# Expert weights of a mixture-of-experts trunk: four buffers each, lower parts written over the loaded weights, 8 KB rows in place of 4 KB

## The chip, the cores and the metric

The kernel runs on one core of a Trainium2 chip. The metric is the time of one execution on the device in microseconds. Lower is better.

## The reference

One layer of a trunk over 512 positions of width 1024, all in float32. First a mixer (gated spatial mixing beside latent attention), then a mixture of experts. The change lies in the second part:

```python
def moe_ffn(h, w_router, router_bias, w_gate, w_up, w_down, ws_gate, ws_up, ws_down):
    ...                               # sigmoid scores, best 4 of 8 groups, then the best 8 of 64 experts per token
    combine = ...                     # (512, 64): weight of each expert for each token, zero where it isn't chosen
    routed = jnp.zeros_like(t)
    for e0 in range(0, N_EXPERTS, EXPERT_BLOCK):
        sl = slice(e0, e0 + EXPERT_BLOCK)
        hg = jnp.einsum('nd,edf->nef', t, w_gate[sl])
        hu = jnp.einsum('nd,edf->nef', t, w_up[sl])
        hw = jax.nn.silu(hg) * hu * combine[:, sl, None]
        routed = routed + jnp.einsum('nef,efd->nd', hw, w_down[sl])
    shared = (jax.nn.silu(t @ ws_gate) * (t @ ws_up)) @ ws_down
    return (routed + shared).reshape(B, S, D)
```

Each of the 64 experts has a gate and an up matrix of 1024 x 256 and a down matrix of 256 x 1024, 1 MB each, so 192 MB of weights are read once. With 8 experts for each of 512 tokens an expert has 64 tokens on average.

## The kernel before

The engines run programs of their own and meet at semaphores. The first part of the kernel (to about 300 us) is the mixer. Then comes the router on VectorE (DVE) with the shared expert between its steps, and then the expert loop, `every_expert`: four steps written out, a loop of 14 turns with four steps each, and four steps written out. A step handles expert E and prepares E+1 and E+2.

**Weights.** SyncE (SP) loads them, in the order of its program. For each expert there are six transfers of 512 KB: gate and up for the first four chunks of the contraction (half 0), gate and up for the other four (half 1), and two for down. Each fills 128 partitions with rows of 4096 bytes that are contiguous in memory. There are two buffers for each (`w_gu[half][i]`, `w_d[i]`). A load for E waits until VectorE has made the lower part of expert E-2, the last reader of the buffer (`gu_low_ok`, `d_low_ok`).

**Split operands.** A float32 product is made of three passes in a faster format. ScalarE (ACT) copies a weight to its high part (`gate_up_high`, `down_high`), VectorE subtracts it from the weight for the low part (`gate_up_low`, `down_low`, all through `lowered` at line 1503), and TensorE (PE) adds high x high, high x low and low x high (`three_passes`, lines 574 to 576). The high and the low parts have one buffer per half, and both engines wait for the matmuls that read it (`gu_mm0`, `gu_mm`, `d_mm`). Rows, hidden values and weights all go this way. Per expert VectorE makes six low parts of weights, two of rows (`xeT_low`) and one of hidden values (`hwT_low`), the gated product (line 1527) and two output pieces (`oute`, line 1539).

**Rows.** GpSimd (POOL) gathers an expert's token rows from memory by a list (line 524; `xe`, four buffers; up to 128 rows of 4352 bytes, the rest of the list out of bounds and skipped), and scatters the outputs with addition into the result (line 530; `oute`, two buffers; rows of 4096 bytes). Its program is: for each e, gather(e+3), wait for `oute_ok`, wait for `st_y` of all scatters before, scatter(e). As two experts may add to one row, a scatter begins only after the one before it has landed. Before the loop it also stores x, with the shared expert's output added, as the rows to add to (`st_x`).

**TensorE's step.** Transposes of the hidden values of E (line 827), `gate_up` for E+1, the transposes of the gathered rows for E+2 (`rows_T`, line 810), `down` for E.

Weights go through DMA queue q1 (SP's), gathers and scatters through q0 (POOL's), on the same 16 DMA engines.

Of the kernel before, what the change touches and what calls it, by code (L numbers as in the profile page):

```python
# [22 lines left out]
F32 = mybir.dt.float32  # L23
# [23 lines left out]
def trunk_kernel(nc, a, out):  # L47
# [31 lines left out]
    with ExitStack() as ctx:  # L79
# [106 lines left out]
        hwT_high = at("hwT_high", 183, [P, FC, P], F32R)  # L186
        hwT_low = at("hwT_low", 184, [P, FC, P], F32R)
# [14 lines left out]
        def small(name, shape, dt=F32):  # L202
# [63 lines left out]
        (consts, dve_step, pool_step, silu_c, rs_ok, col_ok, col_mm, ada_dve, acc_ok, ada_mm, mod_ok, g1_ok,  # L266
         g2_ok, ss_ok, std_ok, h_ok, hT_tr, hT_raw, hT_ok, wsT_tr, wsT_ok, proj_mm, proj_ok) = (sem(n) for n in (
            "consts", "dve_step", "pool_step", "silu_c", "rs_ok", "col_ok", "col_mm", "ada_dve", "acc_ok", "ada_mm",
            "mod_ok", "g1_ok", "g2_ok", "ss_ok", "std_ok", "h_ok", "hT_tr", "hT_raw", "hT_ok", "wsT_tr", "wsT_ok", "proj_mm", "proj_ok"))
        (stats_ok, vstats_ok, vstd_ok, lstd_ok, lrstd_ok, latn_ok, latT_tr, latT_ok, v_ok, gate_mm, gate_ok, kpe_ok, up_mm, up_ok, sq_ok,  # L270
         ssq_ok, qstd_ok, ang_ok, trig_ok, qk_ok, qkT_tr, qkT_ok) = (sem(n) for n in (
            "stats_ok", "vstats_ok", "vstd_ok", "lstd_ok", "lrstd_ok", "latn_ok", "latT_tr", "latT_ok", "v_ok", "gate_mm", "gate_ok", "kpe_ok",
            "up_mm", "up_ok", "sq_ok", "ssq_ok", "qstd_ok", "ang_ok", "trig_ok", "qk_ok", "qkT_tr", "qkT_ok"))
        (s_mm, nmax_ok, exp_ok, pT_tr, pT_ok, av_mm, o_ok, mix_v, oss_ok, ostd_ok, orstd_ok, mix_ok, mixT_tr, out_mm,
         x1_ok, ss2_ok, std2_ok, h2_ok, st_h2, h2T_tr, h2T_ok, rt_mm, sco_ok, selm_ok, pos_mm, lmat_ok, list_mm,
         list_ok) = (sem(n) for n in (
            "s_mm", "nmax_ok", "exp_ok", "pT_tr", "pT_ok", "av_mm", "o_ok", "mix_v", "oss_ok", "ostd_ok", "orstd_ok", "mix_ok",
            "mixT_tr", "out_mm", "x1_ok", "ss2_ok", "std2_ok", "h2_ok", "st_h2", "h2T_tr", "h2T_ok", "rt_mm",
# [5 lines left out]
        ld_gu = [[sem(f"ld_gu{half}_{i}") for i in range(2)] for half in range(2)]  # L284
        ld_d = [sem("ld_d0"), sem("ld_d1")]
# [10 lines left out]

        def num(E, d=0):
            m, r = E
            return r + d if m is None else m * 4 + (r + d)

        def pairs(E, d=0):

            m, r = E
            return r // 2 + 1 + d if m is None else m * 2 + (r // 2 + 1 + d)
# [12 lines left out]
        def first(E):  # L317

            return E[0] is None and E[1] == 0

# [54 lines left out]
        EXTRA0 = NE // 2  # L375
# [8 lines left out]
        def _(sp):  # L384
# [73 lines left out]
            def extra(i):  # L458
# [3 lines left out]
                load_gate_up(e, 0, 0)  # L462
                load_gate_up(e, 0, 1)
# [107 lines left out]
        def _(pe):  # L571
# [241 lines left out]
            def gate_up(i, n, before):  # L813
                pe.wait_ge(xe_low_ok, times(n, 2) + 2)
                wait(pe, hw_ok, before)
                for half in range(2):
                    pe.wait_ge(gu_low_ok[half], n + 1)
                    for c in range(HC):
                        last = three_passes(bank[2 + i][:], xeT_high[i][:, half * HC + c, :], xeT_low[i][:, half * HC + c, :],
                                            gu_high[half][:, :, c, :], gu_low[half][:, :, c, :], half == 0 and c == 0, half == 1 and c == HC - 1)  # L820
# [9 lines left out]
            def down(n):  # L830
# [3 lines left out]
                for m in range(2):  # L834
                    cols = slice(m * BANK, (m + 1) * BANK)
                    for j in range(FC):
                        last = three_passes(bank[4 + m][:], hwT_high[:, j, :], hwT_low[:, j, :], d_high[:, j, cols], d_low[:, j, cols], j == 0, j == FC - 1)
# [5 lines left out]
            def gate_up_of(E):  # L843
                gate_up(E[1] % 2, num(E), num(E, -1))
# [46 lines left out]
            def step(E):  # L891
# [6 lines left out]
                down(num(E))  # L898
# [3 lines left out]
            def extra(i):  # L902
# [4 lines left out]
                gate_up(0, n, n)  # L907
                hidden_T(0, n)
                down(n)
# [5 lines left out]
        def _(act):  # L915
# [20 lines left out]
            act.wait_ge(rs_ok, 1)  # L936
# [736 lines left out]
```

## Time and profile before

| | |
|---|---|
| median of 3 runs | 1065.07 us |
| lowest, highest | 1056.51, 1077.57 us |
| profiled execution, first to last instruction (span) | 1060.5 us |
| PE, DVE, ACT, POOL busy | 953.4, 880.5, 611.8, 273.5 us |
| moved by DMA | 286.27 MB, mean 270 GB/s |
| mean granted TensorE clock | 0.960 of full |

The profile is of one execution. Busy time is the time in which an engine works on an instruction. The chain of waits is followed back from the last instruction to what released it, step by step. "Idle before" is the engine's idle time just before an instruction, and the releaser is what ended it. The DMA share is the mean over the 16 DMA engines of the share of time in which they handle packets. It can be a little over 1, and a full one doesn't tell whether more bytes could move.

### The profile page before, as it was taken

The numbers are of one execution on the slowest core, as the hardware profiler recorded it, in microseconds if no ns is written. First come the engines' busy times: TensorE is split into PE (matmuls) and PEld (weight loads), VectorE is DVE, ScalarE is ACT, GpSimd is POOL, SyncE is SP. The second block draws the span as 40 slices with busy tenths as digits, with TensorE's granted clock in tenths as the row PEclk, the third lists the DMA queues.
The fourth block names the chain that finished last, engine by engine and source line by source line (L and its number), as shares of the span: only waits on it lengthen the run. The fifth ranks groups of instructions, "written<-read, shape, count | busy, mean of one in ns | idle before, by whom it ended". The sixth has DMA issues, their size and how long they took to land.

```text
span 1060.5 us, 14279 instructions
## 1 busy us (share of the span) xinstructions
PE 953.4 (90%) x4323; PEld 744.9 (70%) x4324; DVE 880.5 (83%) x1276; ACT 611.8 (58%) x961; POOL 273.5 (26%) x181
## 2 busy tenths in 40 slices
PE   1899999997999889999999999999998999899895
PEld 1654665876887568777778777787776777777773
DVE  4887775354548779999999999999998999999994
ACT  4215443554022157777777777776776777777672
POOL 1000205400000103242433423343333233333231
PEclk9899999588998999999999999999999999999998
DMA  9995222000044488999999999999999999999982
GB/s 351 396 381 206 80 79 109 1 1 1 40 178 184 132 308 286 368 368 340 342 357 344 370 352 342 361 349 359 322 345 353 314 345 365 360 359 352 358 290 48
DMA packets 93682, 286.27 MB, mean 270 GB/s; under 512 B 19497, under 2 KB 20009, under 8 KB 92753
## 3 DMA queue, kind: packets, MB, share of 16 engines
q1 hardware_dynamic: 71424, 248.04, 62.5%
q0 software_dynamic: 19056, 36.89, 13.9%
q10 hardware_dynamic: 3168, 0.94, 0.4%
q8 instruction: 16, 0.26, 0.1%
q14 instruction: 18, 0.14, 0.0%
HBM read 282.50 MB, written 37.88 MB: 302 GB/s over the span
## 4 chain that ended last, share of the span: by engine, by line
DMA 43%; PE 33%; DVE 11%; issue 8%; ACT 3%; POOL 1%; POOLq 0%; SPq 0%; DVEq 0%; ACTq 0%
DMA out<-oute,src_tab 31%; PE bank L613 9%; DMA xe<-h_rows,src_tab 6%; DMA w_gu<-in_w_exp_up 5%; PE bank L574 4%; PE bank L576 4%; PE bank L575 4%; DVE gu_low L1503 4%; PE bank L698 2%; PE bank L777 2%; PE bank L715 2%; DVE oute L1539 2%; POOL out L530 1%; DMA x_sb<-in_x 1%; PE bank L794 1%
## 5 line engine op out<-in xcount | busy, mean ns | idle before, releaser
L1503 DVE TENSOR_TENSOR gu_low<-w_gu,gu_high 128x1024 fp32r<-128x1024 f32 x256 | 301.6, 1221 | 9.7 <-ACT gu_high L1115 5.4
L1115 ACT CAST gu_high<-w_gu 128x1024 fp32r<-128x1024 f32 x256 | 256.7, 1055 | 76.4 <-PE bank L576 49.7
L530 POOL DMA_INDIRECT out<-oute,src_tab x64 | 133.2, 2081 | 426.7 <-DMA out<-oute,src_tab 291.1
L574 PE MATMUL bank<-gu_high,xeT_high 128*128 128x512 f32 x512 | 208.4, 407 | 4.5 <-DVE xeT_low L1503 4.2
L576 PE MATMUL bank<-gu_high,xeT_low 128*128 128x512 f32 x512 | 202.1, 395 | 0.0
L575 PE MATMUL bank<-gu_low,xeT_high 128*128 128x512 f32 x512 | 201.8, 394 | 0.0
L1503 DVE TENSOR_TENSOR d_low<-w_d,d_high 128x1024 fp32r<-128x1024 f32 x128 | 150.6, 1220 | 0.0
L1121 ACT CAST d_high<-w_d 128x1024 fp32r<-128x1024 f32 x128 | 128.3, 1056 | 12.9 <-PE bank L576 12.0
L574 PEld LDWEIGHTS bank<-gu_high,xeT_high 128*128 128x128 f32 x512 | 97.0, 189 | 26.3 <-issue 3.9
L574 PE MATMUL bank<-d_high,hwT_high 128*128 128x512 f32 x256 | 109.2, 427 | 6.7 <-DVE hwT_low L1503 6.5
L524 POOL DMA_INDIRECT xe<-h_rows,src_tab x64 | 100.6, 1571 | 53.2 <-DVE src_tab L1575 27.8
L576 PEld LDWEIGHTS bank<-gu_high,xeT_low 128*128 128x128 f32 x512 | 96.6, 189 | 22.4
L575 PEld LDWEIGHTS bank<-gu_low,xeT_high 128*128 128x128 f32 x512 | 96.9, 189 | 19.8 <-issue 0.2
L810 PE MATMUL bank<-ident,xe 128*128 128x128 f32 x512 | 70.8, 281 | 40.5 <-DMA xe<-h_rows,src_tab 38.4
L810 PEld LDWEIGHTS bank<-ident,xe 128*128 128x128 f32 x512 | 63.5, 192 | 58.7 <-issue 54.3
L576 PE MATMUL bank<-d_high,hwT_low 128*128 128x512 f32 x256 | 104.0, 406 | 0.0
L575 PE MATMUL bank<-d_low,hwT_high 128*128 128x512 f32 x256 | 102.9, 402 | 0.0
L1503 DVE TENSOR_TENSOR xeT_low<-bank,xeT_high 128x512 fp32r<-128x512 f32 x128 | 82.3, 685 | 21.4 <-ACT xeT_high L1131 20.2
L1131 ACT CAST xeT_high<-bank 128x512 fp32r<-128x512 f32 x128 | 68.8, 590 | 52.1 <-PE bank L810 50.0
L1539 DVE TENSOR_TENSOR oute<-bank,mod_rows 128x512 f32<-128x512 f32 x128 | 82.2, 685 | 8.6 <-PE bank L576 8.6
L574 PEld LDWEIGHTS bank<-d_high,hwT_high 128*128 128x128 f32 x256 | 50.3, 196 | 16.0 <-DVE d_low L1503 4.6
L576 PEld LDWEIGHTS bank<-d_high,hwT_low 128*128 128x128 f32 x256 | 49.7, 194 | 11.6
(283 smaller groups left out, 1277.1 us busy)
## 6 DMA issues: line engine op xcount, KB each, us to landing
w_gu<-in_w_exp_gate SPq DMA_DIRECT2D x128, 512.0 KB
w_gu<-in_w_exp_up SPq DMA_DIRECT2D x128, 512.0 KB
w_d<-in_w_exp_down SPq DMA_DIRECT2D x128, 512.0 KB
ada_w<-in_w_ada SPq DMA_DIRECT2D x8, 2048.0 KB
first_w<-in_w_ada SPq DMA_DIRECT2D x3, 2048.0 KB, 22.9
w_out_sb<-in_w_out SPq DMA_DIRECT2D x2, 2048.0 KB, 7.3
w_lat_sb<-in_w_in SPq DMA_DIRECT2D x1, 2688.0 KB, 23.2
x_sb<-in_x SPq DMA_DIRECT2D x1, 2048.0 KB, 13.7
```

The lines of the kernel that those rows point to most:

```text
L524: pool.indirect_dma_start(xe[i][:], None, h2_dram, bass.IndirectOffsetOnAxis(ap=rows, axis=0), bounds_check=last_row, oob_is_err=False).th ...
L530: pool.indirect_dma_start(out_rows, bass.IndirectOffsetOnAxis(ap=rows, axis=0), oute[i][:], None, bounds_check=last_row, oob_is_err=False, ...
L574: pe.matmul(dst, xh, wh, start=start, stop=False)
L575: pe.matmul(dst, xh, wl, start=False, stop=False)
L576: return pe.matmul(dst, xl, wh, start=False, stop=stop)
L613: last = pe.matmul(bank[2 + i % 4][:, 0:n1 - n0], hT[:, c, t * P:(t + 1) * P], w[:, c, n0:n1], start=(c == 0), stop=(c == C - 1))
L810: last = pe.transpose(bank[c // 4][:, c % 4 * P:(c % 4 + 1) * P], xe[b][:, c:D:C], ident[:])
L1115: act.copy(gu_high[half][:, m], w_gu[half][i][:, m]).then_inc(gu_high_ok[half], 1)
L1121: act.copy(d_high[:, m], w_d[i][:, m]).then_inc(d_high_ok, 1)
L1131: act.copy(xeT_high[i][:, m * HC:(m + 1) * HC, :], bank[m][:].rearrange("p (c n) -> p c n", c=HC)).then_inc(xe_high_ok, 1)
L1503: return dve.tensor_tensor(low, whole, high.bitcast(F32), ALU.subtract)
L1539: last = dve.tensor_tensor(oute[i][:, cols], bank[4 + m][:], mod[:, GATE2, cols], ALU.mult)
```

## The change

1. Each expert weight gets four buffers in place of two. One buffer `w_gu[i]` (16 KB per partition) holds gate and up whole; the four lie at 40, 56, 80 and 0 KB. The last is the place of x, so SyncE waits before the first load into it for the stores of x (`st_x`) and for the shared expert's last matmuls (`sd_mm`). `w_d[i]` lie at 72, 102, 120 and 175.5 KB. The one at 120 waits for `sgu_mm`, the one at 175.5 for `sd_mm`.
2. The low part is written over the loaded weight (`gu_low[i]` and `d_low[i]` have the addresses of `w_gu[i]` and `w_d[i]`), and the matmuls read it there. So a buffer is free only when the matmuls have read it: a load for E waits for `gu_mm` or `d_mm` of expert E-4.
3. Three transfers of 1 MB with rows of 8192 bytes per expert in place of six of 512 KB with rows of 4096 bytes.
4. VectorE no longer waits for `gu_mm0`, `gu_mm` and `d_mm` before a low part. The high parts keep one buffer per half and their waits.
5. To free semaphores, those of the square roots and reciprocals of the first part are merged into `std_ok` and `rstd_ok`, with the same order. TensorE's `gate_up` and `down` and the waits of ACT take the new buffer numbers (E % 4).

The core of the diff (left out: the merged semaphores, the numbers passed on, and the branch for more than 128 tokens in an expert):

```diff
         HC = C // 2
-        w_gu = [[at(f"w_gu{half}_{i}", 40 + 16 * half + 8 * i, [P, 2, HC, FF]) for i in range(2)] for half in range(2)]
-        w_d = [at(f"w_d{i}", 72 + 8 * i, [P, FC, D]) for i in range(2)]
-        gu_high = [at(f"gu_high{half}", kb, [P, 2, HC, FF], F32R) for half, kb in enumerate((16, 88))]
-        gu_low = [at(f"gu_low{half}", kb, [P, 2, HC, FF], F32R) for half, kb in enumerate((24, 102))]
+        D_AT = (72, 102, 120, 175.5)
+        GU_AT = (40, 56, 80, 0)
+        def gate_and_up(name, i, dt):
+            return at(f"{name}{i}", GU_AT[i], [P, 2, C, FF], dt)
+        w_gu = [gate_and_up("w_gu", i, F32) for i in range(4)]
+        gu_low = [gate_and_up("gu_low", i, F32R) for i in range(4)]
+        half_of = [slice(0, HC), slice(HC, C)]
+        w_d = [at(f"w_d{i}", kb, [P, FC, D]) for i, kb in enumerate(D_AT)]
+        d_low = [at(f"d_low{i}", kb, [P, FC, D], F32R) for i, kb in enumerate(D_AT)]
+        gu_high = [at(f"gu_high{half}", kb, [P, 2, HC, FF], F32R) for half, kb in enumerate((16, 24))]
         d_high = at("d_high", 112, [P, FC, D], F32R)
-        d_low = at("d_low", 120, [P, FC, D], F32R)
...
-            def load_gate_up(e, i, half):
+            def load_gate_up(e, i):
                 for m, w in enumerate(("w_exp_gate", "w_exp_up")):
-                    src = a[w][0, bass.ds(e, 1)].rearrange("o (p c) n -> p (o c) n", c=C)[:, half * HC:(half + 1) * HC, :]
-                    sp.dma_start(w_gu[half][i][:, m], src).then_inc(ld_gu[half][i], 16)
+                    src = a[w][0, bass.ds(e, 1)].rearrange("o (p c) n -> p (o c) n", c=C)
+                    sp.dma_start(w_gu[i][:, m], src).then_inc(ld_gu[i], 16)
             def load_down(e, i):
-                src = a["w_exp_down"][0, bass.ds(e, 1)].rearrange("o (p c) n -> p (o c) n", c=FC)
-                for j in range(FC):
-                    sp.dma_start(w_d[i][:, j], src[:, j]).then_inc(ld_d[i], 16)
+                sp.dma_start(w_d[i][:], a["w_exp_down"][0, bass.ds(e, 1)].rearrange("o (p c) n -> p (o c) n", c=FC)).then_inc(ld_d[i], 16)
             def down_step(E):
-                wait(sp, d_low_ok, num(E, -1))
+                wait(sp, d_mm, num(E, -3))
                 apart(sp, "sp")
-                load_down(num(E), E[1] % 2)
+                load_down(num(E), E[1] % 4)
             def step(E):
-                for half in range(2):
-                    wait(sp, gu_low_ok[half], num(E, -1))
-                    apart(sp, "sp")
-                    load_gate_up(num(E), E[1] % 2, half)
-                if not (E[0] is None and E[1] == 0):
+                if unrolled(E, 3):
+                    sp.wait_ge(sgu_mm, T)
+                    down_step((None, 2))
+                    sp.wait_ge(st_x, 16 * T)
+                    sp.wait_ge(sd_mm, T)
+                wait(sp, gu_mm, num(E, -3))
+                apart(sp, "sp")
+                load_gate_up(num(E), E[1] % 4)
+                if not (unrolled(E, 0) or unrolled(E, 3)):
                     down_step(after(E, -1))
...
             def gate_up_high(half, i, loads, n):
-                act.wait_ge(ld_gu[half][i], loads)
+                act.wait_ge(ld_gu[i], loads)
                 wait(act, (gu_mm0, gu_mm)[half], n)
                 for m in range(2):
-                    act.copy(gu_high[half][:, m], w_gu[half][i][:, m]).then_inc(gu_high_ok[half], 1)
+                    act.copy(gu_high[half][:, m], w_gu[i][:, m, half_of[half]]).then_inc(gu_high_ok[half], 1)
...
             def gate_up_low(half, i, n):
-                wait(dve, (gu_mm0, gu_mm)[half], n)
                 for m in range(2):
                     dve.wait_ge(gu_high_ok[half], times(n, 2) + (m + 1))
-                    last = lowered(gu_low[half][:, m], w_gu[half][i][:, m], gu_high[half][:, m])
+                    last = lowered(gu_low[i][:, m, half_of[half]], w_gu[i][:, m, half_of[half]], gu_high[half][:, m])
                 last.then_inc(gu_low_ok[half], 1)
             def down_low(i, n):
-                wait(dve, d_mm, n)
                 for m in range(2):
                     dve.wait_ge(d_high_ok, times(n, 2) + (m + 1))
-                    last = lowered(d_low[:, m], w_d[i][:, m], d_high[:, m])
+                    last = lowered(d_low[i][:, m], w_d[i][:, m], d_high[:, m])
                 last.then_inc(d_low_ok, 1)
```

## Rows read from the trace of the kernel before

**Rows 1.** Page, part 2: busy tenths of 40 equal slices.
```profile
DVE  4887775354548779999999999999998999999994
...
DMA  9995222000044488999999999999999999999982
```

**Rows 2.** Windows: busy us (instructions) of PE, PEld, DVE, ACT, POOL; PEclk, DMA share, GB/s.
```profile
500.00:620.00 120.00, 114.53 (x547) 93.41 (x547) 118.85 (x144) 90.46 (x131) 47.42 (x24) 1.00 1.00 354
...
740.00:860.00 120.00, 109.85 (x511) 89.39 (x509) 111.41 (x134) 84.82 (x123) 40.50 (x23) 0.97 0.99 335
860.00:980.00 120.00, 111.45 (x529) 91.20 (x529) 114.81 (x139) 86.95 (x128) 42.57 (x24) 0.99 1.02 358
```

**Rows 3.** Timeline of POOL: start us, us, instruction [idle before, releaser].
```profile
380.56 1.04 POOL L524 DMA_INDIRECT xe<-h_rows,src_tab  x1 [3.16 <-DMA out<-x_sb]
399.29 1.79 POOL L530 DMA_INDIRECT out<-oute,src_tab  x1 [17.68 <-DVE oute L1539]
...
604.92 2.87 POOL L530 DMA_INDIRECT out<-oute,src_tab  x1 [6.13 <-DVE oute L1539]
...
615.85 1.87 POOL L530 DMA_INDIRECT out<-oute,src_tab  x1 [6.00 <-DMA out<-oute,src_tab]
...
1028.94 1.84 POOL L530 DMA_INDIRECT out<-oute,src_tab  x1 [6.54 <-DMA out<-oute,src_tab]
...
1054.64 1.55 POOL L530 DMA_INDIRECT out<-oute,src_tab  x1 [6.87 <-DVE oute L1539]
```

**Rows 4.** Timeline of DVE: start us, us, instruction.
```profile
421.52 0.42 DVE L1503 TENSOR_TENSOR hwT_low<-bank,hwT_high 128x256 fp32r<-128x256 f32 x1
...
431.44 0.42 DVE L1503 TENSOR_TENSOR hwT_low<-bank,hwT_high 128x256 fp32r<-128x256 f32 x1
```

**Rows 5.** Waits, 400 to 1060 us: us in total, times, longest us.
```profile
POOL out L530 <- DMA out<-oute,src_tab: 291.1, 44, 8.4
POOL out L530 <- DVE oute L1539: 118.9, 18, 17.7
...
PE bank L810 <- DMA xe<-h_rows,src_tab: 38.4, 31, 3.2
...
ACT gu_high L1115 <- DMA w_gu<-in_w_exp_up: 20.3, 9, 3.1
```

**Rows 6.** Chain that ended last, in order of time: start us, us, what.
```profile
604.92 10.12 DMA out<-oute,src_tab
...
1011.32 18.25 DMA w_gu<-in_w_exp_up
```

**Rows 7.** Waits of SP's queue, 420 to 1060 us.
```profile
SPq L330 <- DVE gu_low L1503: 274.4, 114, 6.0
```

**Rows 8.** Windows of one us, at 309, 714, 715, 708 and 1058 us.
```profile
309.00:310.00 1.00, 1.00 (x11) 1.00 (x11) 0.96 (x2) 0.50 (x2) 0.00 (x0) 1.00 1.07 426
...
714.00:715.00 1.00, 1.00 (x6) 0.81 (x5) 1.00 (x2) 1.00 (x2) 0.00 (x0) 1.00 1.00 275
715.00:716.00 1.00, 1.00 (x6) 0.82 (x5) 1.00 (x2) 0.50 (x2) 0.00 (x0) 1.00 1.07 287
...
708.00:709.00 1.00, 1.00 (x6) 0.65 (x4) 1.00 (x2) 0.57 (x1) 1.00 (x1) 1.00 1.03 422
...
1058.00:1059.00 1.00, 0.00 (x0) 0.00 (x0) 0.00 (x0) 0.00 (x0) 0.00 (x0) 0.50 0.63 119
```

**Rows 9.** DMA view: packets of queue q0; issues of gathers and scatters.
```profile
q0 software_dynamic: 19056, 36.89, 13.9%
...
xe<-h_rows,src_tab POOLq DMA_INDIRECT x64
out<-oute,src_tab POOLq DMA_INDIRECT x64
```

**Rows 10.** Window from 332 to 358 us.
```profile
332.00:358.00 26.00, 23.10 (x85) 15.40 (x84) 19.63 (x56) 1.02 (x3) 1.27 (x2) 0.87 0.00 1
```

**Rows 11.** Timeline of SP's queue at the first load of expert 3.
```profile
380.48 0.33 SPq L435 DMA_DIRECT2D w_gu<-in_w_exp_gate  x1
```

More of the change, by code:

```diff
@@ L283, in trunk_kernel @@
             "sgu_mm", "ssilu_ok", "shw_ok", "shT_tr", "shT_ok", "sd_mm", "sh_ok"))
-        ld_gu = [[sem(f"ld_gu{half}_{i}") for i in range(2)] for half in range(2)]
-        ld_d = [sem("ld_d0"), sem("ld_d1")]
+        ld_gu = [sem(f"ld_gu{i}") for i in range(4)]
+        ld_d = [sem(f"ld_d{i}") for i in range(4)]
         ld_xe = [sem(f"ld_xe{i}") for i in range(4)]
@@ L319, in first, with unrolled @@
             return E[0] is None and E[1] == 0
+        def unrolled(E, r):
+            return E[0] is None and E[1] == r
         def wait(eng, s, value):
@@ L374, in trunk_kernel @@
         NI = T * H
-        EXTRA0 = NE // 2
+        EXTRA0 = NE // 4
         HW = HC // 2
@@ L828, in hidden_T, with down @@
                 last.then_inc(hwT_tr, 1)
-            def down(n):
+            def down(slot, n):
                 pe.wait_ge(d_low_ok, n + 1)
@@ L836, in down @@
                     for j in range(FC):
-                        last = three_passes(bank[4 + m][:], hwT_high[:, j, :], hwT_low[:, j, :], d_high[:, j, cols], d_low[:, j, cols], j == 0, j == FC - 1)
+                        last = three_passes(bank[4 + m][:], hwT_high[:, j, :], hwT_low[:, j, :], d_high[:, j, cols], d_low[slot][:, j, cols], j == 0, j == FC - 1)
                 last.then_inc(d_mm, 1)
@@ L897, in step @@
                     rows_T_of(after(E, 2))
-                down(num(E))
+                down(E[1] % 4, num(E))
             every_expert(pe, step)
@@ L985, in _ @@
             act.wait_ge(stats_ok, 1)
-            act.activation(latss[:, :, 0], latss[:, :, 0], ACT.Sqrt, bias=epsc[:], scale=1.0 / QL).then_inc(lstd_ok, 1)
-            act.activation(latss[:, :, 1], latss[:, :, 1], ACT.Sqrt, bias=epsc[:], scale=1.0 / KL).then_inc(lstd_ok, 1)
-            act.wait_ge(lrstd_ok, 1)
+            act.activation(latss[:, :, 0], latss[:, :, 0], ACT.Sqrt, bias=epsc[:], scale=1.0 / QL).then_inc(std_ok, 1)
+            act.activation(latss[:, :, 1], latss[:, :, 1], ACT.Sqrt, bias=epsc[:], scale=1.0 / KL).then_inc(std_ok, 1)
+            act.wait_ge(rstd_ok, RSTD_LAT)
             for t in range(T):
@@ L1015, in _ @@
             act.wait_ge(vstats_ok, 1)
-            act.activation(lnmv[:, :, 1], lnmv[:, :, 1], ACT.Sqrt, bias=epsc[:]).then_inc(vstd_ok, 1)
+            act.activation(lnmv[:, :, 1], lnmv[:, :, 1], ACT.Sqrt, bias=epsc[:]).then_inc(std_ok, 1)
             act.wait_ge(kpe_ok, T)
@@ L1035, in _ @@
             act.wait_ge(ssq_ok, 2 * T)
-            act.activation(qkss[:], qkss[:], ACT.Sqrt, bias=epsc[:], scale=1.0 / QD).then_inc(qstd_ok, 1)
+            act.activation(qkss[:], qkss[:], ACT.Sqrt, bias=epsc[:], scale=1.0 / QD).then_inc(std_ok, 1)
             act.wait_ge(g1_ok, 1)
@@ L1070, in _ @@
             act.wait_ge(oss_ok, 1)
-            act.activation(oss[:], oss[:], ACT.Sqrt, bias=epsc[:], scale=1.0 / GW).then_inc(ostd_ok, 1)
-            act.wait_ge(orstd_ok, 1)
+            act.activation(oss[:], oss[:], ACT.Sqrt, bias=epsc[:], scale=1.0 / GW).then_inc(std_ok, 1)
+            act.wait_ge(rstd_ok, RSTD_OUT)
             for t in range(T):
@@ L1081, in std2 @@
                 act.wait_ge(ss2_ok, t + 1)
-                act.activation(ss[:, t:t + 1], ss[:, t:t + 1], ACT.Sqrt, bias=epsc[:], scale=1.0 / D).then_inc(std2_ok, 1)
+                act.activation(ss[:, t:t + 1], ss[:, t:t + 1], ACT.Sqrt, bias=epsc[:], scale=1.0 / D).then_inc(std_ok, 1)
             for t in range(T - 1):
@@ L1143, in gate_up_high_of @@
             def gate_up_high_of(half, E):
-                gate_up_high(half, E[1] % 2, times(pairs(E), 32), num(E))
+                gate_up_high(half, E[1] % 4, times(fours(E), 32), num(E))
             def down_high_of(E):
-                down_high(E[1] % 2, times(pairs(E), 16 * FC), num(E))
+                down_high(E[1] % 4, times(fours(E), 16), num(E))
             def rows_high_of(E):
@@ L1252, in _ @@
             dve.tensor_scalar(turns[:], turns[:], -1.0, float(np.pi / 2), ALU.mult, ALU.add).then_inc(ang_ok, 1)
-            dve.wait_ge(std_ok, 1)
-            dve.reciprocal(ss[:], ss[:]).then_inc(rs_ok, 1)
+            dve.wait_ge(std_ok, STD_X)
+            dve.reciprocal(ss[:], ss[:]).then_inc(rstd_ok, 1)
             for n in range(1, ADA_FIRST):
@@ L1301, in _ @@
                     dve.tensor_copy(ws_raw[:], bank[6][:].rearrange("p (g n) -> p g n", g=GG)).then_inc(wsT_ok, 1)
-            dve.wait_ge(lstd_ok, 2)
-            dve.reciprocal(latss[:], latss[:]).then_inc(lrstd_ok, 1)
+            dve.wait_ge(std_ok, STD_LAT)
+            dve.reciprocal(latss[:], latss[:]).then_inc(rstd_ok, 1)
             for j in range(ADA_FIRST + T + 1, ADA):
@@ L1323, in _ @@
             last.then_inc(vstats_ok, 1)
-            dve.wait_ge(vstd_ok, 1)
+            dve.wait_ge(std_ok, STD_V)
             link(dve.reciprocal(lnmv[:, :, 1], lnmv[:, :, 1]))
@@ L1397, in _ @@
             outputs(T - 1)
-            dve.wait_ge(ostd_ok, 1)
-            dve.reciprocal(oss[:], oss[:]).then_inc(orstd_ok, 1)
-            dve.wait_ge(orstd_ok, 1)
+            dve.wait_ge(std_ok, STD_OUT)
+            dve.reciprocal(oss[:], oss[:]).then_inc(rstd_ok, 1)
+            dve.wait_ge(rstd_ok, RSTD_OUT)
             for t in range(T):
@@ L1424, in norm2 @@
             def norm2(t):
-                dve.wait_ge(std2_ok, t + 1)
+                dve.wait_ge(std_ok, STD_X2 + t)
                 link(dve.reciprocal(ss[:, t:t + 1], ss[:, t:t + 1]))
@@ L1542, in gate_up_low_of @@
             def gate_up_low_of(half, E):
-                gate_up_low(half, E[1] % 2, num(E))
+                gate_up_low(half, E[1] % 4, num(E))
             def rows_low_of(E):
```

50 lines of the change are left out of this document (24 added, 26 removed).

## The prediction

> **What bounds the kernel now.** I read the page first, then windows of the expert loop, then the waits, then the order of time on GpSimd, on VectorE and on TensorE. The expert loop is the long stage: its 64 scatters begin at 399.29 us, and the last of them ends the program [rows 3]. On the page two resources look full there: DVE shows nines, and so does DMA [rows 1]. Windows of 120 us between 500 and 980 make that finer: VectorE is busy for 111 to 119 us of each, and the DMA share stands at 0.99 to 1.02 while 335 to 358 GB/s move [rows 2]. Busy shares alone don't tell which one decides, so I went to the distances between starts.
>
> The 61 scatter starts from 399.29 to 1028.94 us are 60 intervals [rows 3]: 629.65/60 = 10.49 us per expert. VectorE by itself could do better: in a stretch in which nothing stalls it, one hwT_low starts 9.92 us after the one before [rows 4]. So about 0.57 us of each interval is not VectorE's. The waits say whose it is. The scatter waits for the scatter before it 44 times (291.1 us), and only 18 times for VectorE's result. TensorE waits for gathered rows 31 times (38.4 us). The weights are late only 9 times, 20.3 us on ACT [rows 5].
>
> The order on GpSimd shows the mechanism. Scatters add into the same output rows, so each one waits until the one before has landed; those at 604.92 and 615.85 us are 10.93 us apart, and the second was waiting for the first. The gather that feeds an expert three places later stands behind the scatter in the same program, so when the scatter is late the gather is too [rows 3]. There the chain of waits spends 10.12 us from a scatter's issue to its landing [rows 6]. At the end of the kernel, where no weights flow, the last scatter starts at 1054.64 us and the span ends at 1060.5 us, 5.86 us later. So the same transfer costs 4.26 us more beside the weight loads. This chain, not VectorE, is what sets the loop in 44 of its steps.
>
> **The change, part by part.** *Six transfers to three, 4 KB rows to 8 KB rows.* The bytes are the same, 3 MB per expert. SyncE issues three instructions fewer per expert, worth nothing: it waits 274.4 us in the loop for VectorE to free gate and up buffers alone [rows 7]. What a row costs on a DMA engine: at full rate 4 KB rows moved at 422 GB/s, 26.4 GB/s per engine, so 0.155 us each; the shared expert's 8 KB rows moved at 426 GB/s, so 0.308 us each [rows 8]. Per expert that is 48 x 0.155 = 7.44 us against 24 x 0.308 = 7.39 us of each engine: a gain of 0.05 us, even if the loads were what is late. A half-size transfer is thus no handicap once others stand behind it.
>
> The other side of the larger rows is who stands behind them. Scatter and gather go through GpSimd's queue q0, weights through q1, on the same 16 engines. The DMA view counts 19056 packets on q0 for 64 gathers and 64 scatters [rows 9] and the five plain stores that GpSimd issues: 143.3 per transfer, 9 per engine. How the two queues share an engine shows in the scatter's dip. A scatter alone moves 119 GB/s at a DMA share of 0.63, so 189 GB/s while busy, and one of its 4 KB rows takes 0.347 us. If one weight packet went between two scatter packets, a pair of 8 KB would take 0.502 us and the rate would be 261 GB/s; with two weight packets per scatter packet it would be 299, and with scatters let past 189. In the dip at 714 to 716 us, 275 and 287 GB/s are measured at a share of 1.00 to 1.07 [rows 8]. One for one is nearest. Then every q0 packet waits for one weight packet, and doubling that packet adds 9 x 0.153 = 1.37 us to each scatter, and as much to a gather.
>
> The Trainium skill (DMA: Bandwidth & Descriptors, the section Queues, rings and completion order) says the same: a DMA engine goes round its queues packet by packet, whatever a packet holds. It speaks against this change. By that rule the added wait is the same 1.37 us; by a split in bytes it would be nothing.
>
> Bounds of that price: below, 0 (the engine shares by bytes, or the wait lies elsewhere). Above, the whole excess of a scatter beside the loads doubles, 4.26 us (everything the loads do to it grows with their packet). I take 1.37 because the dip fits it. A relief comes off: the DMA share is about 1.0 of 10.49 us [rows 2]; with nearly the same work in 11.7 us it is about 0.88, so 12% of the packets meet no weight packet. Of 2 x 1.37 us this is 0.33. Net 1.04 us.
>
> It counts where a scatter waits for a scatter: 44 x 1.04 = 46 us. The 18 steps that wait for VectorE hide it in their slack; without that cover they would add up to 19 us more.
>
> *Four buffers per weight, lower parts over the loaded weights.* A gate/up load of an expert is released by the matmuls of the expert four back instead of by VectorE's low part of the expert two back; the down load likewise. That is about one step earlier. It can only repair waits for weights: 20.3 us on ACT, and those overlap the gathers' lateness. With 44 scatter-bound steps the gain is from 0 to 20 us; I take 0, as these steps stay bound. At the start two more loads (gate and up of expert 2, down of expert 1; 3 MB) go out in the pause from 332 to 358 us, in which 1 GB/s moves [rows 10]. Nobody waits for them in the first experts, so 0; at most the 3.15 MB/354 GB/s = 9 us that they take off the DMA engines later. Against it, expert 3's load now waits for x to be stored (GpSimd passes the same wait at 380.56 us [rows 3]) and for the shared expert's end. In the kernel before its first half was issued at 380.48 us [rows 11], so the time is the same, and the cost 0. Behind that wait in SyncE's queue stand only loads of expert 3 and later.
>
> *Removed waits on VectorE.* Its low parts no longer wait for the matmuls (gu_mm0, gu_mm, d_mm). The high part, for which VectorE waits anyway, still waits for the same matmuls, so nothing moves; VectorE's operations keep their count and sizes. Writing the result over one operand has no row here: bounded by nothing and, upwards, by one per cent of 6 x 1.2 us, 0.07 us per expert; taken as 0. The matmuls read low parts with another stride: 0, since their columns are as many. The merged semaphores (std_ok, rstd_ok) keep the same waits: 0.
>
> **The sum.** 1060.5 + 46 = 1106.5 us on the profiled execution's span. That span lies 4.6 us below the median of the runs, 1065.1 us. So 1111 us.
>
> **The rivals.**
> *Faster: DMA work, not latency, is the bound, and lead and larger rows buy it.* For: a DMA share near 1.0 in every window, 18.25 us from issue to landing for a load near the end [rows 6]. Against: the saving in engine time is 0.05 us per expert, and what is late in the middle is the gather. If it were so, VectorE's 9.92 us would be the floor: 60 x 0.57 = 34 us less, 1031 us. It decides only if q0's packets aren't delayed by more than 0.6 us per scatter. 15%.
> The Trainium skill (the same page, the section Bandwidth) advises transfers of 1 MiB and more for 75% of the peak; by that rule the new loads would be the better ones, and this rival would gain. The trace disagrees for queued loads: half-megabyte ones moved 422 GB/s.
> *No change: the engines share by bytes.* Then scatter and gather see the same wait, and the lead saves from 0 to 17 us: 1048 to 1068 us. For: the rates of the dip lie a little over 261. Against: they are nearer to it than to anything else. 23%.
> *Much slower: the weight queue gets a fixed number of packets ahead, not one.* Then all 4.26 us doubles. With weights flowing 80% of the time an interval is 5.86 + 0.8 x 8.5 + 0.75 = 13.4 us, 60 x 2.9 = 175 us in all: 1240 us. Against: the one-for-one dip. 7%.
> The forecast itself: 55%, with its own range from 1085 to 1150 us (a net price of 0.5 us in 44 steps to 1.4 us in 60).
>
> **How the numbers follow.** Chances: forecast 55, much slower 7, no change 23, faster 15. Within 2% (1044 to 1086 us) is about what measurement can tell from no change. "Much slower" and nearly all of the forecast lie above 1086: 0.60. The faster rival gives 0.12 below 1044, and 0.03 above for a part of its gain. The rest, 0.28, is the same. The range leaves out the much slower case and the lower part of the faster one: 1040 to 1155 us.
>
> **What would show it.** Right: scatter starts about 11.5 us apart; waits of scatter for scatter above 44; the links from a scatter to its landing near 11.5 us in place of 10.12; more wait of TensorE for gathered rows than 38.4 us; no wait for weights; VectorE busy for less than 110 us in 120; the dips at a higher rate, near 16 x 12.3 KB/0.655 us = 300 GB/s, and longer. Wrong: landing links that stay at 10 us, or intervals near 9.9 us with VectorE never waiting. The weakest step is the one-for-one sharing, which rests on rates alone; next comes the count of steps that the scatter binds.

## The result, and the profile after

The changed kernel takes 1098.9 us (median of 6 runs, 1091.0 to 1109.6) against 1068.5 us before in the same comparison: ratio 1.030, 95% interval 1.021 to 1.039. It is slower. The profiled execution has a span of 1107.8 us; it is one of the longer ones (the shortest has 1089.2), as are those of the runs below with 2 KB rows, with gathers earlier and 8 KB rows, and with two chains, so the waits shown for these are somewhat larger than in a typical run.

The page's busy tenths, beside [rows 1]: eights now stand among the nines of VectorE and of DMA.

```profile
DVE  4888773445568788989989989798988988798794
...
DMA  9995122000192699998989989988989999989952
```

The four windows (columns as in [rows 2]):

```profile
500.00:620.00 120.00, 106.53 (x509) 86.54 (x508) 110.62 (x133) 84.99 (x122) 41.68 (x22) 1.00 0.91 324
620.00:740.00 120.00, 107.72 (x493) 87.85 (x493) 107.26 (x129) 81.81 (x119) 40.26 (x22) 0.94 0.92 317
740.00:860.00 120.00, 105.38 (x480) 85.96 (x480) 106.32 (x127) 80.73 (x115) 38.67 (x21) 0.96 0.92 324
860.00:980.00 120.00, 104.25 (x474) 84.60 (x474) 103.86 (x124) 77.97 (x113) 37.48 (x22) 0.94 0.92 319
```

VectorE is busy for 104 to 111 us of 120 where it was 111 to 119, and the DMA share is 0.91 to 0.92 where it was 0.99 to 1.02. Neither is full any more. The starts on GpSimd, beside [rows 3]:

```profile
399.44 1.78 POOL L541 DMA_INDIRECT out<-oute,src_tab  x1 [18.99 <-DVE oute L1548]
...
696.82 2.87 POOL L541 DMA_INDIRECT out<-oute,src_tab  x1 [6.13 <-DVE oute L1548]
699.99 1.75 POOL L535 DMA_INDIRECT xe<-h_rows,src_tab  x1 [0.30 <-issue]
711.54 2.27 POOL L541 DMA_INDIRECT out<-oute,src_tab  x1 [9.80 <-DMA out<-oute,src_tab]
...
1076.42 2.87 POOL L541 DMA_INDIRECT out<-oute,src_tab  x1 [6.14 <-DVE oute L1548]
```

From 399.44 to 1076.42 us are again 60 intervals: 676.98/60 = 11.28 us, where it was 10.49. From the first of these starts to the last is 47.3 us longer than before, and the spans differ by 47.3 us, so all of the loss of the profiled execution is in these intervals. The waits of the loop, beside [rows 5]:

```profile
POOL out L541 <- DVE oute L1548: 232.8, 33, 19.0
POOL out L541 <- DMA out<-oute,src_tab: 229.0, 29, 9.8
...
PE bank L821 <- DMA xe<-h_rows,src_tab: 75.7, 36, 5.0
DVE xeT_low L1514 <- ACT xeT_high L1142: 66.9, 40, 4.9
```

The same view of the kernel before has this for VectorE's wait, a row that was not shown ahead:

```profile
DVE xeT_low L1503 <- ACT xeT_high L1131: 19.6, 24, 2.8
```

TensorE's wait for gathered rows rose from 38.4 to 75.7 us. VectorE's wait for the high rows, which are made from these, rose from 19.6 to 66.9 us: 47.3 us more, as much as the span grew. The 20.3 us in which ACT waited for weights are gone. But scatters wait for scatters in fewer steps than before, 29 in place of 44. A row of VectorE's timeline shows one stall, a row of the chain what lies behind it (start, us, what), and a window of one us TensorE's clock in it (columns as in [rows 2]):

```profile
716.80 1.29 DVE L1514 TENSOR_TENSOR xeT_low<-bank,xeT_high 128x512 fp32r<-128x512 f32 x2 [4.05 <-ACT xeT_high L1142]
```

```profile
699.99 13.88 DMA xe<-h_rows,src_tab
```

```profile
714.00:715.00 1.00, 0.86 (x4) 0.90 (x5) 0.00 (x0) 0.19 (x1) 0.88 (x1) 0.50 1.04 434
```

The gather that starts at 699.99 us needs 13.88 us to land, at 713.87. Eight transposes and ACT's copy later, at 716.80 us, VectorE goes on; it had been idle for 4.05 us. The scatter issued just ahead of it in the same queue, at 696.82 us, took 13.9 us to land; the next scatter, which waited for it, starts at 711.54 us.

The late gather also costs clock. TensorE was idle for 3.82 us before these transposes, and by then its granted clock had fallen to 0.50, the lower of its two levels; it stayed there to 720 us. The eight transposes took 1.94 us, against 1.13 us for eight of them in the kernel before (at 720.85 us), so 0.8 us of this stall is clock. From 400 to 1040 us the clock is at 0.50 for 47.8 us in all, where it was 13.7 us before. Over the whole run the transposes' busy time rose from 70.8 to 78.0 us. So the clock makes the stalls longer, by 7 us in the transposes, well below the loss. Of the runs below, the one with 8 KB rows and two buffers has the clock at 0.50 for 56.0 us, and all others for 8.8 to 17.1 us.

### The profile page after: what moved, and what is told of

Same layout as the page of the kernel before. It is cut to its first block, busy times and chain, and to the rows that moved or that the text cites. A ratio compares the mean times of both kernels' runs of the same rounds, so it can differ in the third digit from the quotient of the medians.

```text
span 1107.8 us, 13597 instructions
## 1 busy us (share of the span) xinstructions
PE 967.5 (87%) x4323; PEld 756.8 (68%) x4324; DVE 883.0 (80%) x1276; ACT 614.3 (55%) x961; POOL 272.1 (25%) x181
## 3 DMA queue, kind: packets, MB, share of 16 engines
q0 software_dynamic: 19056, 36.89, 14.0%
## 4 chain that ended last, share of the span: by engine, by line
PE 41%; DMA 32%; DVE 14%; issue 6%; ACT 4%; POOL 3%; POOLq 0%; DVEq 0%; SPq 0%; ACTq 0%
DMA out<-oute,src_tab 16%; DMA xe<-h_rows,src_tab 14%; PE bank L624 9%; PE bank L585 6%; PE bank L586 6%; PE bank L587 6%; DVE gu_low L1514 6%; POOL out L541 3%; PE bank L821 3%; PE bank L709 2%; DVE oute L1548 2%; PE bank L788 2%; PE bank L726 2%; ACT gu_high L1126 1%; PE bank L805 1%
## 5 line engine op out<-in xcount | busy, mean ns | idle before, releaser
L821 PE MATMUL bank<-ident,xe 128*128 128x128 f32 x512 | 78.0, 300 | 76.1 <-DMA xe<-h_rows,src_tab 75.7
L821 PEld LDWEIGHTS bank<-ident,xe 128*128 128x128 f32 x512 | 68.4, 196 | 95.3 <-issue 93.2
L585 PE MATMUL bank<-d_high,hwT_high 128*128 128x512 f32 x256 | 114.2, 446 | 6.6 <-DVE hwT_low L1514 6.4
L587 PE MATMUL bank<-d_high,hwT_low 128*128 128x512 f32 x256 | 107.4, 420 | 0.0
L586 PE MATMUL bank<-d_low,hwT_high 128*128 128x512 f32 x256 | 106.8, 417 | 0.0
L585 PEld LDWEIGHTS bank<-d_high,hwT_high 128*128 128x128 f32 x256 | 53.9, 210 | 16.9 <-DVE d_low L1514 4.6
L587 PEld LDWEIGHTS bank<-d_high,hwT_low 128*128 128x128 f32 x256 | 52.1, 204 | 12.5
## 6 DMA issues: line engine op xcount, KB each, us to landing
w_gu<-in_w_exp_gate SPq DMA_DIRECT2D x64, 1024.0 KB, 7.4
w_gu<-in_w_exp_up SPq DMA_DIRECT2D x64, 1024.0 KB, 10.8
w_d<-in_w_exp_down SPq DMA_DIRECT2D x64, 1024.0 KB, 9.1
first_w<-in_w_ada SPq DMA_DIRECT2D x3, 2048.0 KB, 22.8
x_sb<-in_x SPq DMA_DIRECT2D x1, 2048.0 KB, 13.7
```

What stands on the lines that cost most here:

```text
L585: pe.matmul(dst, xh, wh, start=start, stop=False)
L586: pe.matmul(dst, xh, wl, start=False, stop=False)
L587: return pe.matmul(dst, xl, wh, start=False, stop=stop)
L821: last = pe.transpose(bank[c // 4][:, c % 4 * P:(c % 4 + 1) * P], xe[b][:, c:D:C], ident[:])
```

## The experiments

**The transfers alone.** Four buffers, releases and in-place lower parts stay; only the transfers are cut in two again, which halves their rows too. This and the next run make a square of two buffers or four with rows of 4 KB or 8 KB. (Left out of this diff, and of the later ones that cut transfers: ACT's counts of landed transfers and the line that names `src`.)

```diff
-                    sp.dma_start(w_gu[i][:, m], src).then_inc(ld_gu[i], 16)
+                    for c0 in range(0, C, C // 2):
+                        sp.dma_start(w_gu[i][:, m, c0:c0 + C // 2], src[:, c0:c0 + C // 2]).then_inc(ld_gu[i], 16)
...
-                sp.dma_start(w_d[i][:], ...).then_inc(ld_d[i], 16)
+                for j in range(FC):
+                    sp.dma_start(w_d[i][:, j], src[:, j]).then_inc(ld_d[i], 16)
```

> The changed kernel with its weights loaded again in six transfers of 512 KB with rows of 4096 bytes; four buffers, releases and in-place low parts stay. Theory of the row size (each gather and scatter packet waits for one weight packet): the loss goes away, ratio to before 0.99 to 1.01, about 1065 us, and TensorE's wait for gathered rows falls from 75.7 us to about 40 us or less. Rival, the later and bunched release of the four buffers (3 MB within 4 us of each step): the loss stays, ratio about 1.03, about 1099 us, wait for rows about 75 us.

Measured: 1060.6 us, ratio 0.996 (0.991 to 1.001). Its waits:

```profile
PE bank L824 <- DMA xe<-h_rows,src_tab: 40.6, 29, 3.6
...
DVE xeT_low L1517 <- ACT xeT_high L1145: 25.2, 25, 3.2
```

The wait for rows is back at 40.6 us, and VectorE's at 25.2. The loss is gone with the 8 KB rows in 1 MB transfers, so the rival, the later and bunched release, falls. The size of a row and of its transfer change together, here and in all runs below, so these times don't tell one from the other.

**Large rows with two buffers.** The kernel before with one tile for gate and up, loaded whole once both halves' low parts are made; down comes in one transfer too (left out below).

```diff
-                for half in range(2):
-                    wait(sp, gu_low_ok[half], num(E, -1))
-                    apart(sp, "sp")
-                    load_gate_up(num(E), E[1] % 2, half)
+                for half in range(2):
+                    wait(sp, gu_low_ok[half], num(E, -1))
+                apart(sp, "sp")
+                load_gate_up(num(E), E[1] % 2)
```

> The kernel before with three transfers of 1 MB with rows of 8192 bytes; two buffers and separate low parts stay, and gate and up of an expert are released together, after the second half's low part. Theory of the row size: ratio 1.03 or more, about 1100 us, with TensorE's wait for gathered rows near 75 us in place of 38.4 us. Rival, the four buffers' release: ratio about 1.00. If weights now come late, since the first half's lead is lost, ACT waits for w_gu for more than the 20.3 us of before; then part of a loss is that.

Measured: 1104.9 us, ratio 1.034 (1.025 to 1.044).

```profile
POOL out L529 <- DMA out<-oute,src_tab: 331.4, 47, 8.5
...
PE bank L809 <- DMA xe<-h_rows,src_tab: 66.1, 29, 6.0
DVE xeT_low L1502 <- ACT xeT_high L1130: 58.9, 27, 6.3
...
ACT gu_high L1114 <- DMA w_gu<-in_w_exp_up: 12.1, 8, 2.0
```

TensorE's wait for rows is 66.1 us, a little under the 75 us that were expected. This profile is of an execution of typical length (span 1097.8 us), and VectorE's wait for rows and the span have grown by nearly the same here too, 39.3 and 37.3 us.

But the path is not quite that of the changed kernel. Scatters wait for scatters in 47 steps, not 29, and scatters make up 79% of the chain of waits from 500 to 900 us, where they are 29% in the changed kernel and 67% in the kernel before. The starts of scatters are 11.16 us apart, 0.67 us more than before.

The square is complete: 4 KB rows give 1.000 and 0.996, 8 KB rows 1.034 and 1.030, whatever the number of buffers. The late weights are not behind it: ACT waits for them for 12.1 us, less than in the kernel before. At 4 KB, four buffers, in-place low parts and releases at the matmuls together are worth between nothing and 1%.

**A third size.** The changed kernel with twelve transfers of 256 KB and rows of 2048 bytes.

```diff
-                    sp.dma_start(w_gu[i][:, m], src).then_inc(ld_gu[i], 16)
+                    for c0 in range(0, C, C // 4):
+                        sp.dma_start(w_gu[i][:, m, c0:c0 + C // 4], src[:, c0:c0 + C // 4]).then_inc(ld_gu[i], 16)
...
```

> The changed kernel with its weights loaded in twelve transfers of 256 KB with rows of 2048 bytes. Theory of one weight packet between two of the other queue: the wait per gather and scatter halves once more against 4 KB rows (about 0.7 us less each), and TensorE's wait for rows falls below 30 us (40.6 with 4 KB rows, 75.7 with 8 KB); the time gains at most 15 us on the 4 KB kernel, 1045 to 1060 us. Against it works the cost of smaller rows: if the weights then come late (ACT waits for w_gu), it is slower than with 4 KB rows, 1065 to 1100 us. Rival, the 8 KB rows cost through something that only they have: the wait for rows stays at about 40 us.

Measured: 1061.0 us, ratio 0.998 (0.992 to 1.004).

```profile
ACT gu_high L1130 <- DMA w_gu<-in_w_exp_up: 122.5, 37, 4.9
...
DVE gu_low L1518 <- ACT gu_high L1130: 29.9, 27, 2.3
...
PE bank L825 <- DMA xe<-h_rows,src_tab: 3.3, 7, 0.8
```

The wait for rows is 3.3 us, so the series over 2, 4 and 8 KB is 3.3, 40.6 and 75.7 us. The rival, that only 8 KB rows have a price, falls. What the shorter wait gives is taken back: ACT now waits 122.5 us for weights, and VectorE 29.9 us for what ACT makes of them, more than the 25.2 us that it waited for rows with 4 KB. So the time is that of 4 KB rows, just above the 1045 to 1060 us expected of the theory and below the 1065 to 1100 us expected with late weights.

**Hardly any weights.** From the third expert on, the loads of the kernel before bring 512 bytes per row. The rest of a buffer keeps older weights, so the kernel leaves most of the weights out and its output is not the reference's.

```diff
+                    if not full:
+                        dst, src = dst[:, 0, 0:128], src[:, 0, 0:128]
```

> The kernel before with its loads from the third expert on cut to 512 bytes per row (the rest of a buffer keeps the weights of an earlier expert, so the output is not the reference's). Both theories: no weight traffic beside gathers and scatters, so a scatter lands in 6 to 8 us, no wait for rows, and the intervals are VectorE's own 9.92 us: 60 x 0.57 = 34 us less, about 1030 us, ratio 0.965. If the intervals stay above 10.2 us, the 0.57 us per expert isn't the weights' doing at all.

Measured: 1024.0 us, ratio 0.965 (0.960 to 0.970). A window, with VectorE never idle at 95 GB/s:

```profile
740.00:860.00 120.00, 117.19 (x558) 96.34 (x557) 120.00 (x146) 91.88 (x134) 54.95 (x25) 1.00 0.44 95
```

The starts of scatters are 9.96 us apart. So nearly all of the 0.57 us per expert above VectorE's own 9.92 are the weight traffic's doing, 60 x 0.57 = 34 us as worked out. The view of the tile `xe` (first fence of each pair) and of the tile `oute` (second) gives the time from issue to landing of gathers and scatters from 500 to 900 us (for the kernel before it gives none). With hardly any weights:

```profile
DMA to landing us min/median/max: 4.7/5.3/6.5
```

```profile
DMA to landing us min/median/max: 5.9/6.3/8.5
```

With rows of 2 KB:

```profile
DMA to landing us min/median/max: 6.8/7.7/9.7
```

```profile
DMA to landing us min/median/max: 7.2/8.8/10.6
```

With four buffers and rows of 4 KB:

```profile
DMA to landing us min/median/max: 8.1/9.0/11.7
```

```profile
DMA to landing us min/median/max: 7.7/9.2/12.2
```

With 8 KB, the changed kernel:

```profile
DMA to landing us min/median/max: 7.6/10.9/13.9
```

```profile
DMA to landing us min/median/max: 4.8/9.9/13.9
```

With 8 KB and two buffers:

```profile
DMA to landing us min/median/max: 6.0/8.9/13.2
```

```profile
DMA to landing us min/median/max: 8.8/9.8/11.6
```

In the first four a gather's median goes 5.3, 7.7, 9.0, 10.9 us and a scatter's 6.3, 8.8, 9.2, 9.9 us. The bytes of weights are the same in the last three of these. From 4 to 8 KB the gather grows by 1.9 us and the scatter by 0.7. The two-buffer kernel has the scatter's growth (9.8 us) but not the gather's: its median is 8.9 us, though its longest is 13.2 us where 4 KB rows have 11.7. So the gather's larger growth is not the row size's alone. The records of the packets show the part in which the rows themselves move. From its first row to its last, the median gather takes 3.5 us in the kernel before and 4.4 us with 8 KB rows and two buffers; with four buffers it takes 3.2 and 4.8 us. For scatters it is 3.6 and 4.0 us, and 4.0 and 4.1 us. So gathers are stretched in both 8 KB kernels, and scatters by less.

**Gathers earlier.** If it is the late gather that costs, an earlier one should pay it back, with the 8 KB rows kept.

```diff
-            for e in range(3):
+            for e in range(4):
...
-                g = e + 3
+                g = e + 4
                 if g < NE:
-                    if e:
-                        pool.wait_ge(xeT_tr, e)
-                        pool.wait_ge(w_ok, e)
+                    pool.wait_ge(xeT_tr, e + 1)
+                    pool.wait_ge(w_ok, e + 1)
```

> The changed kernel with each gather one expert earlier in GpSimd's program: gather(e+4) ahead of the wait for the output of e, four gathers ahead of the loop. Rows, buffers and scatters as they are. Theory of late gathers (the loss is gathered rows that land late, 75.7 us of wait of TensorE): that wait falls below 20 us and the time to about 1050 us, ratio 0.98 to 0.99. Rival, the chain of scatters itself binds: the wait for rows goes to other places, and the time stays near 1099 us, with a scatter waiting for a scatter in more than 29 steps.

Measured: 1056.9 us, ratio 0.989 (0.982 to 0.996), against 1.030 without the edit.

```profile
DVE oute L1547 <- DMA out<-oute,src_tab: 25.7, 22, 2.8
PE bank L820 <- DMA xe<-h_rows,src_tab: 25.5, 23, 2.3
...
DVE xeT_low L1513 <- ACT xeT_high L1141: 0.4, 1, 0.4
```

VectorE's wait for rows falls from 66.9 to 0.4 us, and the time by 42 us. TensorE still waits 25.5 us, where less than 20 us was expected; VectorE's 0.4 us shows that little of it reaches VectorE. TensorE's clock is at 0.50 for 8.8 us from 400 to 1040 us, in place of 47.8 us. The gathers land no sooner than before, the median still takes 10.9 us: they are only issued sooner. So in the changed kernel the price of the large rows reached the time through the gathers. The same was not tried with 8 KB rows and two buffers, where the chain runs over the scatters. The time is a little short of the forecast 1050: VectorE now waits for a scatter to leave its output buffer, 25.7 us, so the chain of scatters seems to take over.

The same edit in the kernel before, with its two buffers and 4 KB rows:

> The kernel before with each gather one expert earlier in the same way. Theory of late gathers: the 38.4 us wait of TensorE nearly goes, and the time falls by 20 to 35 us, to about 1040 us, ratio 0.97 to 0.98. Rival, the chain of scatters binds in 44 steps: ratio 1.00. Rival, the weights become late instead (2 buffers): ratio 0.99 to 1.00 with ACT waiting for w_gu for well over 20.3 us.

Measured: 1053.3 us, ratio 0.989 (0.983 to 0.995). I had expected 1040 for the theory, and the rival with late weights for 0.99 to 1.00. It is the rival:

```profile
ACT gu_high L1114 <- DMA w_gu<-in_w_exp_up: 93.4, 47, 3.8
...
ACT d_high L1120 <- DMA w_d<-in_w_exp_down: 23.1, 30, 2.8
...
DVE gu_low L1502 <- ACT gu_high L1114: 21.5, 23, 1.7
...
DVE xeT_low L1502 <- ACT xeT_high L1130: 0.5, 2, 0.3
```

Early gathers bring 1.1% and no more: rid of one wait, VectorE meets weights that come late, 93.4 and 23.1 us on ACT and 21.5 us on VectorE. In the kernel before, the gathers' lateness had hidden it.

**What remains with large rows.** To the changed kernel with early gathers, a second chain: odd experts add into a scratch tensor, so their part is missing from the result, and a scatter waits only for the one two back.

```diff
-                pool.indirect_dma_start(out_rows, ...).then_inc(st_y, 16)
+                pool.indirect_dma_start((out_rows, scratch)[i], ...).then_inc((st_y, st_z)[i], 16)
...
-                if e:
-                    pool.wait_ge(st_y, 16 * e)
+                if e >= 2:
+                    pool.wait_ge((st_y, st_z)[e % 2], 16 * (e // 2))
```

> The changed kernel (8192 byte rows) with gathers one expert earlier, and its scatters in two chains: those of odd experts add into a scratch tensor, so half of the routed output is missing and each scatter waits for the one two back only. Theory (with 8 KB rows and early gathers the chain of scatters is what remains): VectorE no longer waits for a scatter's landing (25.7 us before) and the time falls below the 1057 us of the kernel with one chain, to 1035 to 1045 us, ratio 0.97 to 0.98. Rival, DMA throughput binds: no change, ratio 0.985 to 0.995.

Measured: 1035.1 us, ratio 0.973 (0.966 to 0.980). Two of its windows, then its wait for weights:

```profile
740.00:860.00 120.00, 117.12 (x558) 96.28 (x557) 120.00 (x146) 90.77 (x133) 55.07 (x25) 1.00 0.99 366
860.00:980.00 120.00, 111.89 (x530) 90.98 (x529) 113.87 (x138) 86.24 (x129) 47.16 (x24) 1.00 0.99 362
```

```profile
ACT gu_high L1128 <- DMA w_gu<-in_w_exp_up: 45.1, 15, 4.4
```

With neither gather nor scatter in the way, VectorE is busy for all of 120 us up to 860 us, at 366 GB/s.

**Both edits together.** Four buffers, 4 KB rows, early gathers: to the changed kernel, the diffs of the first experiment and of the earlier gathers.

> Four buffers and in-place low parts, six transfers with 4096 byte rows, and each gather one expert earlier. Theory (three separate limits: late gathers, weights late with two buffers, and scatter behind scatter with larger rows): with 4 KB rows the scatters land in about 10 us, gathers are early and weights have four buffers, so no wait of TensorE for rows and none of ACT for weights; intervals of 10.1 to 10.3 us, about 1045 us, ratio 0.975 to 0.985, below both gather4 kernels before. Rival, the 16 DMA engines' throughput binds near 10.4 us per expert: the same as the other two, ratio 0.988 to 0.99, with the wait moved to the scatters.

Measured: 1048.0 us, ratio 0.986 (0.981 to 0.990), between the theory's 0.975 to 0.985 and the rival's 0.988. It leaves nothing out and is faster than the kernel before and the changed one. Beside the 0.989 (0.982 to 0.996) of 8 KB rows with early gathers it shows no difference that these runs can tell: once the gathers are early, the row size has lost its price. Nor does it stand clear of the 0.989 of two buffers with 4 KB rows.

```profile
620.00:740.00 120.00, 117.19 (x557) 96.32 (x556) 120.00 (x146) 91.21 (x133) 51.76 (x24) 1.00 1.00 346
740.00:860.00 120.00, 110.05 (x502) 89.11 (x501) 108.90 (x132) 81.70 (x121) 40.87 (x22) 0.96 0.98 336
```

```profile
ACT gu_high L1128 <- DMA w_gu<-in_w_exp_up: 84.2, 25, 6.0
...
DVE gu_low L1516 <- ACT gu_high L1128: 22.8, 15, 4.3
```

The theory's "no wait for weights" was a miss. From 500 to 740 us VectorE is never idle. Then the DMA share stays at 0.98 while only 336 GB/s move; in all ACT waits 84.2 us for weights and VectorE 22.8 us for ACT, as much as the 21.5 us with two buffers. So more buffers did not do away with late weights, they put them off. An estimate says why: 3.15 MB of weights and about 0.54 MB of rows per expert, at VectorE's 9.92 us, need 372 GB/s. Here 346 GB/s moved from 620 to 740 us, so the lead of the buffers shrank until it was used up. By these rows DMA throughput is the next limit. The kernel with 8 KB rows and two chains moved 366 GB/s from 740 to 860 us, and was late only after that. Whether that comes from the rows or from the other chain was not separated.

## Why the prediction was right

*What bounds the loop.* Right that it is latency on queue q0, not VectorE and not SyncE. The run with hardly any weights gave the floor that was worked out: ratio 0.965, scatters 9.96 us apart. Incomplete in naming the chain of scatters alone: it counted who waited most often on GpSimd. Earlier gathers gave 1.1% in the kernel before and 42 us in the changed one, so the gathers behind the scatters bind as well. With 8 KB rows and two buffers, the chain still ran mostly over scatters, as forecast.

*One weight packet between two of q0.* Right in sign, and near in size on the mean of the two transfers. The new rows of one-us windows (columns as in [rows 8]) and the packets of the queues (packets, MB, share):

```profile
703.00:704.00 1.00, 1.00 (x6) 0.80 (x6) 0.92 (x3) 1.00 (x2) 0.00 (x0) 1.00 0.99 291
704.00:705.00 1.00, 1.00 (x7) 0.88 (x6) 1.00 (x1) 1.00 (x2) 0.00 (x0) 1.00 1.02 303
705.00:706.00 1.00, 1.00 (x6) 0.83 (x5) 1.00 (x2) 1.00 (x2) 0.00 (x0) 1.00 1.02 320
```

```profile
q1 hardware_dynamic: 43776, 248.02, 58.6%
q0 software_dynamic: 19056, 36.89, 14.0%
```

The dip was forecast at 300 GB/s and stands at 291, 303 and 320, where it had been 275 and 287. But each is one dip. The kernel before has 213 GB/s at a share of 1.08 from 701 to 702 us, between one for one and scatters let past, so the rates alone don't show one for one. Nor could they tell turns of one row each from turns of nine packets each, which is what a transfer gives an engine in either queue: the mix of rows, and so the rate, is the same.

The packets of q0 are as many as in [rows 9]; only the weights' packets are fewer and larger. The forecast gave each transfer nine packets per engine as if all were rows, but 36.89 MB in 19056 packets are 1.9 KB each: more than half of the packets of gathers and scatters are of 4 or 8 bytes, and whether such a packet waits for a weight packet too is not shown.

In landing, 1.37 us was forecast for scatter and gather each; the medians moved by 0.7 and 1.9 us, mean 1.3. The split between them was an error, and with 8 KB rows and two buffers the gather's median (8.9 us) is that of 4 KB rows (9.0 us), so one weight packet between two of q0 stays the nearest picture and is not proven. The upper bound, a doubling of the whole excess of 4.26 us, is excluded. That excess itself was one pair of transfers; by the medians beside 4 KB rows and beside hardly any it is 9.2 - 6.3 = 2.9 us.

*How often it counts.* This is the step that failed in its form. It put the price on 44 steps in which a scatter waits for a scatter and expected more of these, with 11.5 us from a scatter to its landing. There are 29 such steps, and the median landing takes 9.9 us, near the 10 us that the forecast had named as a sign of being wrong. In the changed kernel the price came as late gathers: VectorE's 47.3 us of added wait for rows. With two buffers and 8 KB rows, the 47 steps and 0.67 us more per interval are much nearer to the forecast's form. The sum's 46 us are close to the 47.3 us of the profiled spans, yet the medians differ by only 30.4 us. So the term 44 x 1.04 us was too large by half in a typical run, and that the time still came out near the forecast is in part luck. The overlap left out, as the waits suggest, is that a late gather slows VectorE, its output comes later, and the next scatter then finds the one before landed.

*The relief.* A share of 0.88 was forecast for the DMA engines, though 10.49/11.7 is 0.90; 0.91 to 0.92 came. The relief of both transfers was taken off the price of one: 1.37 us less 12% is 1.21, not 1.04. Intervals of 11.5 us were forecast; 11.28 came, and by the medians of the runs (30.4 us in 60 intervals) 11.0.

*Edits costed at nothing.* The square shows them together as -0.4% (-0.9 to +0.1) at 4 KB rows: four buffers, in-place low parts, VectorE's dropped waits, fewer instructions on SyncE, the merged semaphores. They were not tried one by one. ACT's 20.3 us of waiting for weights did vanish, with no effect on the time beyond this, as said; that it lay in the shadow of the gathers is likely, not shown.

*The rivals.* That larger transfers pay falls with both 8 KB kernels. That the engines share by bytes, so that the row of the other queue doesn't matter, falls with the time of both 8 KB kernels and the landings of the three sizes. That many weight packets stand ahead, so that the whole excess doubles, falls with the landing times: medians grew by at most 1.9 us. One rival was not named: that the size of a transfer and not of its row makes the price. The two changed together in every run, so it stays open. The Trainium skill's rule on going round the queues packet by packet (DMA: Bandwidth & Descriptors, Queues, rings and completion order) agrees with the dips of 291 to 320 GB/s, with a caution: a typical packet of the Trainium skill holds 9 to 17 descriptors, while the profile counts each row as a packet. Turns of a whole transfer's eight rows per engine would add 8 x 0.153 = 1.2 us per gather or scatter, near the forecast's 1.37, and no run here tells the two apart. The Trainium skill's advice of 1 MiB and more per transfer (same page, Bandwidth) did not hold beside a second queue, where halves of that size gave the shorter time.

## What to carry to other kernels

Larger rows and transfers of a bulk load can lengthen the small transfers in the other queue of the same engines: here 3 x 1 MB per expert was 3.0% and 3.4% slower than 6 x 512 KB. Where small, dependent transfers run beside a stream of weights, look at their landing times and not only at the stream's rate. First ask what the late transfer stands behind in its own program: issuing it one step earlier gave 42 us with 8 KB rows, about as much as going back to 4 KB rows, and 1.1% with 4 KB rows. A late transfer can also let TensorE's clock fall, so look at the granted clock in the stall. Behind late gathers stood the chain of scatters and late weights, each close to the next, so removing one limit should be tried together with the cover of the next.

## What was not expected

Rows of 2 KB kept gathers so short that no wait of VectorE for rows is left to speak of, but ACT waited 122.5 us for weights; 2 and 4 KB came out alike, 0.998 and 0.996. And a kernel whose DMA share reads 1.0 was not at the limit of bytes: the share was 0.99 to 1.02 at 335 to 358 GB/s in the kernel before, and 0.99 at 366 GB/s with two chains.
